# Eight kilobytes of expert weights loaded in the mixing stage, and another order on TensorE in the last pair of experts

## What is computed

```
z = rmsnorm(x, g_mix) @ w_in                 # 4 parts of 512: conv_v, conv_g, lru_x, lru_g
y = concat(conformer_conv(conv_v, conv_g), rglru(conv4(lru_x)) * gelu(lru_g))
x = x + y @ w_out                            # "mixing stage"
hf = rmsnorm(x, g_ffn)
group = argmax(hf @ w_group); two best of the group's 8 experts by hf @ w_expert
gate = p(group) * p(expert), renormalized over the two
x = x + sum over the 2 experts of gate * (silu(hf @ w1[e]) * (hf @ w3[e])) @ w2[e]
x = x + sigmoid(rmsnorm(x, g_ple) @ w_ple_gate) * rmsnorm(p @ w_ple, g_ple_proj)
out = rmsnorm(x, g_final)
```

## Time and profile before

| | us |
|---|---|
| median of 3 runs | 1229.04 |
| the profiled execution | 1228.61 |
| its span, first to last instruction | 1227.0 |
| TensorE busy | 1190.4 (97%) |
| VectorE busy | 673.6 (55%) |
| ScalarE busy | 504.2 (41%) |
| DMA, mean over the span | 322 GB/s |
| DMA, 760 to 1164 us | 426 GB/s |

### The profile page before, as it was taken

How to read it: one execution, slowest core, us unless ns; L and a number is a source line. 1 busy time by engine, 2 the same in 40 slices (tenths; PEclk the granted TensorE clock), 3 DMA queues, 4 the chain that set the end, 5 groups by cost and what they waited for, 6 DMA issues and landing times.

```text
span 1227.0 us, 16442 instructions
## 1 busy us (share of the span) xinstructions
PE 1190.4 (97%) x6522; PEld 817.3 (67%) x6522; DVE 673.6 (55%) x1206; ACT 504.2 (41%) x779; POOL 53.8 (4%) x103
## 2 busy tenths in 40 slices
PE   6899999999999999999999999999999999999997
PEld 2597688888889877888878786445444444554436
DVE  5599979787889787755466675111211121121126
ACT  1479663344565576443447384111112111111125
POOL 0100001000010000001001100000000000000000
PEclk9999999999999999999999999999999999999999
DMA  9996868887846555856457779999999999999991
GB/s 366 382 351 271 324 211 334 323 319 293 329 162 242 177 228 185 315 189 230 175 224 261 256 303 427 427 425 426 425 426 426 425 428 424 429 423 427 425 421 44
DMA packets 50987, 394.98 MB, mean 322 GB/s; under 512 B 6673, under 2 KB 8913, under 8 KB 11378
## 3 DMA queue, kind: packets, MB, share of 16 engines
q1 hardware_dynamic: 39618, 337.18, 68.5%
q0 software_dynamic: 9072, 53.92, 12.4%
q10 hardware_dynamic: 2240, 3.10, 1.0%
HBM read 390.68 MB, written 3.49 MB: 321 GB/s over the span
## 4 chain that ended last, share of the span: by engine, by line
PE 81%; DVE 8%; DMA 6%; ACT 3%; SPq 1%; issue 1%; DVEq 0%; ACTq 0%
PE psum L1417 16%; PE psum L794 10%; PE psum L787 10%; PE psum L790 10%; PE psum L1460 8%; PE psum L1349 4%; DMA w_odd_next<-in_w 3%; PE psum L860 2%; PE psum L864 2%; PE psum L862 2%; PE psum L1357 2%; DMA w_raw<-in_units 2%; DVE w_parts L2168 2%; PE psum L821 1%; PE psum L1112 1%; PE psum L1124 1%
## 5 line engine op out<-in xcount | busy, mean ns | idle before, releaser
L2168 DVE TENSOR_TENSOR w_parts<-w_raw,w_parts 128x2048 fp32r<-128x2048 f32 x106 | 241.7, 2288 | 69.3 <-ACT w_parts L1550 69.3
L1550 ACT ACTIVATE w_parts<-w_raw 128x2048 fp32r<-128x2048 f32 x106 | 202.2, 1912 | 79.1 <-DMA w_raw<-in_units 79.1
L1417 PE MATMUL psum<-slabs,arena 128*64 128x512 f32 x704 | 196.3, 592 | 1.0 <-DMA w_odd_late<-in_w 1.0
L787 PE MATMUL psum<-w_parts,h_parts 128*128 128x512 f32 x392 | 155.6, 397 | 3.9 <-ACT h_parts L1550 3.7
L790 PE MATMUL psum<-w_parts,h_parts 128*128 128x512 f32 x392 | 153.3, 391 | 0.0
L1550 ACT ACTIVATE arena<-psum 128x512 f32<-128x512 f32 (+1 forms) x59 | 30.0, 510 | 293.3 <-PE psum L1436 140.6
L1417 PEld LDWEIGHTS psum<-slabs,arena 128*64 128x64 f32 x704 | 62.9, 137 | 110.5 <-issue 108.5
L794 PE MATMUL psum<-w_parts,h_parts 128*128 128x512 f32 x392 | 106.1, 393 | 0.1
L2151 DVE CUSTOM_DVE_ANT_0 aring<-aring,cb 128x1024 f32<-128x1024 f32 x80 | 94.6, 1219 | 0.7 <-DMA aring<-in_ada 0.6
L787 PEld LDWEIGHTS psum<-w_parts,h_parts 128*128 128x128 f32 x392 | 73.9, 188 | 20.8 <-issue 3.2
L1417 PE MATMUL psum<-w_odd,arena 128*64 128x512 f32 x192 | 85.1, 593 | 0.4 <-DMA w_odd_next<-in_w 0.4
(11 more groups left out here) (340 smaller groups left out, 1922.9 us busy)
## 6 DMA issues: line engine op xcount, KB each, us to landing
w_raw<-in_units SPq DMA_DIRECT2D x110, 1024.0 KB, 5.1
slabs<-in_w SPq DMA_DIRECT2D x22, 2048.0 KB, 21.5
slabs<-in_w SPq DMA_DIRECT2D x44, 1024.0 KB, 17.1
aring<-in_ada POOLq DMA_DIRECT2D x40, 1024.0 KB, 5.4
arena<-in_w SPq DMA_DIRECT2D x16, 2048.0 KB, 20.6
w_odd<-in_w SPq DMA_DIRECT2D x16, 2048.0 KB, 20.2
w_odd<-in_w SPq DMA_DIRECT2D x24, 1024.0 KB, 24.3
staged<-in_ada SPq DMA_DIRECT2D x8, 1024.0 KB, 18.5
```

Of the source, the lines that this page charges most:

```text
L787: mm(psum[:, bank, :], high(tile, tok), w_hi(k)[:, col:col + 512], start=first and bank not in begun, stop=False, skip_group_check=True)
L1417: ins = nc.tensor.matmul(psum[s * CAP:(s + 1) * CAP, w, :], xe_t[:, kt, s * CAP:(s + 1) * CAP], up_weights(w, s, b, kt), start=kt == 0, st ...
L1550: return nc.scalar.activation(out_ap, in_ap, func, **kw)
L2168: v.tensor_tensor(w_lo(k), raw(k), w_hi(k).bitcast(F32), ALU.subtract).then_inc(w_split, 1)
```

## The change

1. `w3_odd_next` is loaded in the mixing stage: SP issues it behind the 2 MB load of w1 (pair 0, second expert) and ahead of the third unit of `w_out`, behind a new wait for `conv_ready >= CT` (the four conv results). The issue behind `rank_mm` goes.
2. To make room for it, the vectors are put in another order, so that the first 48 columns hold those still needed (g_ple, g_ffn, the conv norm's, lru_w, lru_b); the product of `w_route` and `g_ffn` goes to an array of its own in the router's scratch, `w_routed`, and is formed in the mixing stage (VectorE, ahead of the split of unit `Z_AT + 6`) and no longer in layer 0; `ones_r` is put over the ones of `cst`, and ScalarE copies it behind the square root of the conv norm.
3. In the last pair only, the scatter of the pair before stands ahead of the up products, and the gate transposes stand where the scatter was, ahead of the activation's transposes and no longer behind the wait for ScalarE's copy. The order of the other pairs stays.

```diff
-VECS = [("g_ple", KT), ("g_ffn", KT), ("g_mix", KT), ("b_ada", 96), ("ln_g", 32), ("ln_b", 32), ("subln_g", 1),
-        ("conv_b", 4), ("conv_ln_g", 4), ("conv_ln_b", 4), ("lru_w", CT * LRU_W), ("lru_b", 4),
-        ("b_r", 4), ("b_i", 4), ("lam", 4)]
+VECS = [("g_ple", KT), ("g_ffn", KT), ("conv_ln_g", 4), ("conv_ln_b", 4), ("lru_w", CT * LRU_W), ("lru_b", 4),
+        ("g_mix", KT), ("b_ada", 96), ("ln_g", 32), ("ln_b", 32), ("subln_g", 1),
+        ("conv_b", 4), ("b_r", 4), ("b_i", 4), ("lam", 4)]
...
+        cst_from = place[0]
         cst = kept("cst", [P, 2 * P])
+        ones_r = at("ones_r", cst_from / 1024 + 0.5, [P, P], F32R)
...
-        ones_r = w_forget_parts[:, :, :, :].rearrange("p a k n -> p (a k n)")
...
-        vec_kept = 4 * 2 * KT
+        vec_kept = 4 * 48
...
+        w_routed = rt[:, 108:396].rearrange("p (k n) -> p k n", k=KT)
...
             load_w1_tile(0, 1, 0)
+            sp.wait_ge(conv_ready, CT)
+            load_w3_half(1, 1, 1, 0)
             load_unit(WOUT_AT + 2)
...
-            sp.wait_ge(rank_mm, 1)
-            load_w3_half(1, 1, 1, 0)
...
-                    ins = mm(psum[:, t, 0:36], h_f[:, kt, t * P:(t + 1) * P], w_route[:, kt, :],
+                    ins = mm(psum[:, t, 0:36], h_f[:, kt, t * P:(t + 1) * P], w_routed[:, kt, :],
...
+            def scatter_places(m):
+
+                pe.wait_ge(sgt_c, m)
+                for c in range(2):
+                    pe.wait_ge(y_low[c], m)
+                    ins = scatter(c, False, False)
+                ins.then_inc(scattered, 1)
+
+            def gates_t_tiles(m):
+
+                pe.wait_ge(sg_ready, m)
+                for t in range(TT):
+                    ins = nc.tensor.transpose(psum[:, G, t * P:(t + 1) * P],
+                                              hot_g[:, t, :, :].rearrange("p e c -> p (e c)"), ident)
+                ins.then_inc(sgt_mm, 1)
...
+                if last:
+                    scatter_places(m)
                 pe.wait_ge(gat0_c, m)
...
+                elif last:
+                    gates_t_tiles(m)
                 else:
-                    pe.wait_ge(sgt_c, m)
-                    for c in range(2):
-                        ins = scatter(c, False, False)
-                    ins.then_inc(scattered, 1)
+                    scatter_places(m)
...
-                pe.wait_ge(sg_ready, m)
                 pe.wait_ge(actt_c, m)
                 if not last:
                     gather(1, TR).then_inc(gat1, 1)
                     pe.wait_ge(gat0_c, m + 1)
-                for t in range(TT):
-                    ins = nc.tensor.transpose(psum[:, G, t * P:(t + 1) * P],
-                                              hot_g[:, t, :, :].rearrange("p e c -> p (e c)"), ident)
-                ins.then_inc(sgt_mm, 1)
+                    gates_t_tiles(m)
...
-            A(ones_r, ones, Cp).then_inc(route_consts, 1)
...
             A(rstd[:], half(5, 0), ACT.Sqrt, scale=1.0 / 512, bias=eps_rms).then_inc(conv_act, 1)
+            A(ones_r[:], ones, Cp).then_inc(route_consts, 1)
...
-                    if layer == 0 and g == 6:
-                        v.tensor_tensor(w_route[:], w_route[:], V("g_ffn", 0, KT).unsqueeze(2).to_broadcast([P, KT, 36]),
-                                        ALU.mult).then_inc(route_consts, 1)
...
+            v.tensor_tensor(w_routed, w_route[:], V("g_ffn", 0, KT).unsqueeze(2).to_broadcast([P, KT, 36]),
+                            ALU.mult).then_inc(route_consts, 1)
             split(Z_AT + 6)
```

More of the change, by code:

```diff
@@ L228, in build @@
         head_sq = kept("head_sq", [P, 4, 8])
-        vec_kept = 4 * 2 * KT
+        vec_kept = 4 * 48
+        assert VEC_AT["g_mix"] <= 48
         w3_odd_next = at("w3_odd_next", (vec_from + vec_kept) / 1024, [P, UNIT])
@@ L274, in build @@
         r_rank = by_tile(236, NE + 2)
-        r_first, r_work, r_el = by_tile(304, NE), by_tile(368, NE), by_tile(432, NE)
-        r_ghot, r_gwork, r_pen = by_tile(496, NG), by_tile(504, NG), by_tile(512, NG)
-        r_s = rt[:, 528:576].rearrange("p (n a) -> p n a", a=TT)
+        w_routed = rt[:, 108:396].rearrange("p (k n) -> p k n", k=KT)
+        r_first, r_work, r_el = by_tile(396, NE), by_tile(460, NE), by_tile(524, NE)
+        r_gwork, r_pen = by_tile(588, NG), by_tile(596, NG)
+        r_s = rt[:, 604:652].rearrange("p (n a) -> p n a", a=TT)
         def hf_t(t, kt):
@@ L1387, in _ @@
             mm(psum[:, 1, 64:64 + NE], tri_r[:], hot_m[:, 1, :], start=True, stop=False)
-            mm(psum[:, 1, 64:64 + NE], ones_r, hot_m[:, 0, :], start=False, stop=True)
-            mm(psum[:, 1, 128:128 + NE], ones_r, hot_m[:, 0, :], start=True, stop=False)
-            mm(psum[:, 1, 128:128 + NE], ones_r, hot_m[:, 1, :], start=False, stop=True).then_inc(rank_mm, 1)
+            mm(psum[:, 1, 64:64 + NE], ones_r[:], hot_m[:, 0, :], start=False, stop=True)
+            mm(psum[:, 1, 128:128 + NE], ones_r[:], hot_m[:, 0, :], start=True, stop=False)
+            mm(psum[:, 1, 128:128 + NE], ones_r[:], hot_m[:, 1, :], start=False, stop=True).then_inc(rank_mm, 1)
             for t in range(TT):
```

## The result

The changed kernel takes 1231.33 us, the median of 7 runs (1228.81 to 1235.31), the kernel before 1227.27 beside it on the same chip (1226.69 to 1230.04): ratio 1.0034, 95% interval 1.0025 to 1.0043. It is slower, and it lies 0.3 us beyond the upper end of the predicted range. That range was laid around 1229.04, the median of three runs; against the kernel beside it the change costs 4.1 us, where a gain of 0.2 was forecast.

A forecast was written before the change was run, and what follows sets the result against it. From 760 us TensorE was taken to bound the kernel, its start set by the mixing stage's tight chain. Terms +0.1 (unit), 0 (small moves), -0.33 (last pair) gave -0.2: 1228.8 us from 1229.04, range 1227.6 to 1230.2, with rivals 1226.6 to 1231.0.

The forecast's parts named there:

- the term for the unit's delay: Mixing stage: the megabyte ahead delays the third output unit's landing from 723.32 to 723.4, costing 0.1 us.
- If that engine's lag adds to the lead-in as well: Mixing stage, upper bound for the third output unit: the slowest DMA engine's lag adds, costing up to 2.46 us.
- Rival (b): Mixing stage: third output unit queues behind the megabyte, lands later than 723.7; at worst 1231.2 us; chance 0.12.
- the stock in flight: Start of experts: loads in flight fall from 5.5 to 3.0 us without a bubble, everything behind 2.46 us earlier.
- rival (c): Stream runs dry at 763 us, last-pair weight waits stay, scatter fills them; time as forecast; chance 0.8 shared with forecast.
- The small moves: Router weights' product, copy of the ones and vectors' new order: 0 together, at most 0.45 us either side.
- The last pair: Last pair of experts: new order starts the second products 0.33 us sooner, bounded by 0 and 0.7.
- Rival (a): Last pair: DMA waits go and scatter costs nothing, second products 3.1 us sooner, 1225.9 us; chance 0.08.
- the forecast: Whole kernel: a gain of 0.2 us, to 1228.8 us; chance 0.8 together with the case of the stream running dry.

The follow-up runs named there:

- e1: The changed kernel with the last pair in its old order; 1.0026 of the kernel before.
- e14: The changed kernel with old last pair, third and fourth output units back to back, second half of w1 behind both; third unit lands 7.0 us behind its issue.
- e16: The changed kernel with old last pair and only columns 0 to 1535 of w3_odd_next ahead of the third output unit; that unit lands 7.3 us behind its issue.
- e9: The changed kernel profiled once more, nothing altered; third output unit lands 7.1 us behind its issue.
- e12: The changed kernel timed again, nothing altered; 1.0018 of the kernel before (1.0002 to 1.0034).
- e11: The changed kernel plus ten unread products where TensorE waits for the split of the fourth output unit; 1.0018 of the kernel before (1.0000 to 1.0036).
- e6: The changed kernel with old last pair and the second half of w1 also ahead of the third output unit; that unit lands 7.6 us behind its issue.
- e13: The changed kernel with old last pair, second half of w1 also ahead, third output unit loaded from GpSimd's queue; that unit lands 7.2 us behind its issue.
- e15: The changed kernel with old last pair, third output unit on GpSimd's queue, second half of w1 issued beside it; that unit lands 9.7 us behind its issue.
- e4: The changed kernel with old last pair and w3_odd_next loaded behind the third output unit and second half of w1; 0.9994 of the kernel before.
- e18: The changed kernel with w3_odd_next moved ahead of the 2 MB w1 load, nothing else; 1227.50 us, 1.0000 of the kernel before.
- e3: The kernel before with only the vectors' new order, w_routed and the ones_r copy; 1.0001 of the kernel before.
- e19: The changed kernel with w3_odd_next ahead of the 2 MB w1 load and scatter halves over VectorE's product and ScalarE's copy; 1225.68 us, 0.9984 of the kernel before.
- e2: The kernel before with the changed last pair alone; 0.9993 of the kernel before.
- e8: The changed kernel with old last pair and only half of w3_odd_next ahead of the third output unit; that unit lands 5.1 us behind its issue.
- e10: The changed kernel with w3_odd_next behind the third output unit and the last pair's scatter split around the activation's transposes; 0.9993 of the kernel before.

## Why the prediction was wrong

1. *"For most engines the extra bytes fill 717.0 to 719.4 ... For the slowest engine all of it queues: ... 721.0, and the unit 2.46 behind it, 723.4 ... I take +0.1."* **This is the step that failed:** the term for the unit's delay, +0.1 us, measured +2.7 (landing 7.5 us behind the issue against 4.8). Its first half holds: the megabyte landed 2.5 us behind the unit's issue (721.0 - 718.54 in the prediction, 725.2 - 722.65 in the trace). The unit should have landed 2.46 us behind that; it landed 5.0 behind it (730.1), as it did in e1, e14 and e16 (4.5 to 5.3). I had named this case in the same step ("If that engine's lag adds to the lead-in as well, the cost is up to 2.46") and had given the other reading the weight because it had a landing behind it. But a landing is one number over 16 engines. It can't say how many of them are late or what each does next; the 0.08 of the earlier trace rows said that one or two were still at work, and I took those for harmless. In e14 two engines make the landing; that they are the same ones is not shown.
2. *Rival (b), "if the third output unit lands later than 723.7 ... at worst +2.46 - 0.3: 1231.2"*, chance 0.12, is what came: the landing was 2.7 later by the profile (7.5 against 4.8), TensorE's wait 2.9 against 0.19, B 2.7 longer. Its mechanism, "each 0.1 later is 0.1 at the end", holds over all rows of the table. By the second timing the price is 1.0018, 2.2 us of 1228 (0.2 to 4.2); by the first 4.1 us (3.1 to 5.3), which is 1.6 more than B and C account for (2.69 - 0.20 = 2.5). The repetitions e9 and e12 have 43.3 and 43.5 in B and no such excess, so that 1.6 stays open. It has the size of one fall of TensorE's clock (told at the end), but neither e12's median nor e11's shows it.

The Trainium skill, "DMA: Bandwidth & Descriptors", section "Queues, rings and completion order", was weighed in this step and set aside with the idle engines. It says that an engine takes one ring's descriptors in order, and also that the increment that tells a completion lands only after every earlier write of that engine, across its queues. By the first alone the prediction had 2.46 us, and the change lost 2.2 to 2.7 in B, so the trace agrees in size. It agrees in mechanism only in e6, where the unit lands 2.5 us behind the load ahead; in after it is 5.0 behind it. By the second, a unit in another queue can't be told as landed before the megabyte's last write, 2.3 us behind the unit's issue in e13 and e15. It landed at 7.2 and 9.7, so nothing here speaks against the rule, and it does not explain the rest.

3. *"the stock in flight at 763.22 falls from 5.5 to 3.0 us, which is above zero, so no bubble comes in and everything behind is 2.46 us earlier."* Wrong. Even with the start of the experts on time the stream lost 1.2 us (e4, above), so a stock worked out from a landing is too high. And in after the experts start 2.7 us later against the stream while the next loads still wait for them (they go out at 770.03, 3.7 us behind the first up product, as before), which runs the stock down further. In after, windows at the start of the experts:

```profile
766.30:768.30 2.00, 2.00 (x11) 0.77 (x12) 1.65 (x8) 0.00 (x0) 0.00 (x0) 1.00 1.03 442
768.30:770.30 2.00, 2.00 (x12) 0.62 (x10) 0.60 (x3) 0.00 (x0) 0.00 (x0) 1.00 0.61 262
770.30:772.30 2.00, 2.00 (x12) 0.67 (x10) 0.00 (x0) 0.00 (x0) 0.00 (x0) 1.00 0.59 156
```

In 4 us it moves 4 x 426 - 2 x (262 + 156) = 868 KB less than a full stream, or 2.0 of the 2.46 us. So rival (c), the stream runs dry, was largely true too, in part by the failed step. In the last pair w_odd_next lands 413.2 us behind the first up product (1144.50 + 35.0 - 766.33 = 413.2), against 413.4 before (1138.70 + 34.2 - 759.53); in e18, with the start on time, it is 412.3. As the prediction said of (c), in this kernel it doesn't touch the time, since the scatter stands over it.

4. *The small moves, 0.* Right: e3 is 1.0001 (0.9987 to 1.0015), B and C as before.
5. *The last pair, -0.33.* Right in each of its steps: scatter from the end of the second products, wait for y_lo, no DMA wait, transposes behind VectorE's product, second products behind the copy. From the first up product of the experts to the second products of the last pair it is 423.89 us (766.33 to 1190.22) against 424.07 (759.53 to 1183.60), so 0.2 and not 0.33; C agrees, 467.3 against 467.5. From the second products of the pair before to those of the last pair the steps are each 0.02 to 0.09 longer than taken (7.02, 2.79, 13.88 and 2.35 us against 6.93, 2.77, 13.83 and 2.31). The wait between gate transposes and activation transposes restarts TensorE twice (0.49 and 0.77 us idle).
6. *Rival (a), the halves add up*, needed y_lo by 1164.4 and did not come. The prediction was right that the two halves of the change compete for one wait. e19 shows the way out: not to lay the scatter over the DMA wait, but to let the load take that wait away and to lay the scatter over VectorE and ScalarE.
7. The chances: 0.8 on the forecast rested on the failed step alone. With one or two engines still at work in the earlier trace rows and 15 us of tight chain behind, (b) had deserved at least the same. The range did not hold its own rival either: (b) at worst was 1231.2, the range ended at 1231.0.

## What to carry to other kernels

A load's landing is the time of its slowest engine. Before a load is put ahead of one on the critical path, ask what the slowest engines still have when the critical bytes arrive: if the load ahead has landed within about 1.6 us of the critical issue it cost at most 0.3 us here, from 2.0 us on it cost 2.2 us or more, and issuing the critical load from GpSimd's queue was no way round. A stock of transfers worked out from landings is too high, and it shrinks when the compute behind it starts late. Look for an idle stretch further up, and not for the nearest free place. And where two parts of a change relieve the same wait, lay one of them over another wait.

## What the runs showed of the hardware

**Two engines of 16 can be a whole share behind.** In e14 the last 131 KB of a megabyte came in the last 3 us of 7.0, on two engines. The price of bytes ahead was 0.3 us for half a megabyte and 2.2 to 2.8 for three quarters, one and two; for two it is no more than the queue itself gives, 2.5 us behind the landing of the load ahead.

**TensorE's clock fell for about 3.3 us in some executions and not in others**, of before's kind and of the change's alike. In e2 the gather behind the router ran at 1.2 GHz in part; windows (the clock is the third number from the end) and the timeline's row:

```profile
753.00:754.40 1.40, 1.09 (x7) 0.64 (x6) 1.07 (x6) 0.15 (x2) 0.00 (x0) 1.00 0.99 421
754.40:757.40 3.00, 2.96 (x15) 2.97 (x16) 1.49 (x10) 0.53 (x1) 0.00 (x0) 0.58 1.00 426
757.40:758.40 1.00, 1.00 (x8) 1.00 (x6) 0.46 (x1) 0.75 (x1) 0.00 (x0) 0.55 1.01 426
```

```profile
754.44 5.47 PE L1349 MATMUL psum<-arena,x_tm 128*128 128x128 f32 x32 [0.35 <-DVE arena L2870]
```

The same 32 products took 3.84 us in the chains of before and after; so a fall costs 1.6 us. Ahead of it TensorE had waited 0.8 us for the router's choice and 0.35 us for the gather's operand, in the executions with the fall and without it (before: 0.84 and 0.35). It came in this place in e2, e8, e11 and e19, and some 15 us earlier in e6, e9 and e14, and in e13 and e15, there for some 7 us. In before, after, e1, e3, e4, e10, e12 and e16 to e18 it came in neither place.

The earlier place is where TensorE waits for the split of the fourth unit, 2.4 to 2.9 us when the third unit is late. Of the nine executions with that wait five have the fall there; of the ten without it (e11, where products fill it, among them) none has. So this fall goes with the wait; that the wait causes it is likely and not shown. Four of those ten have the fall at the router instead, and no timing here shows a difference. A single profile can thus be 1.6 us off by the clock alone, which is more than most steps of this change are worth.
